# A fill of rounded products of ones, and a value tile ahead of the norm's product, in the head of a transformer-block kernel

## The reference

```python
def rmsnorm(x, g):
    xf = x.astype(jnp.float32)
    y = xf * lax.rsqrt(jnp.mean(xf * xf, axis=-1, keepdims=True) + EPS)
    return y * g.astype(jnp.float32)

h = rmsnorm(x, norm_attn[layer])
proj = h @ w_in[layer]
q_n, kv_n, g_n, qkv_s, g_m = jnp.split(proj, split_at, axis=-1)
...
# inside nsa_attention: keys and values of the compressed branch,
# an MLP over overlapping blocks of 32 tokens
kc = compress_blocks(k_c, *cmp_k)
vc = compress_blocks(v_c, *cmp_v)
...
bias_c = jnp.moveaxis(tbl[t5_bucket(dist_c)], (2, 3), (0, 1))
```

## Time and profile before

| | |
|---|---|
| time, median of 3 runs | 777.65 us (776.0 to 778.55) |
| the profiled execution's own time | 777.13 us |
| its span, first to last instruction | 775.3 us |
| TensorE busy | 764.9 us, 99% |
| VectorE, ScalarE, GpSimd busy | 498.7, 393.4, 279.6 us |
| share of the chain that ended last | TensorE 92%, VectorE 4%, ScalarE 2% |
| mean granted TensorE clock | 0.996 of 2.4 GHz |

### The profile page before, as it was taken

How to read it: one execution, slowest core, us unless ns; L and a number is a source line. 1 busy time by engine, 2 the same in 40 slices (tenths; PEclk the granted TensorE clock), 3 DMA queues, 4 the chain that set the end, 5 groups by cost and what they waited for, 6 DMA issues and landing times.

```text
span 775.3 us, 11284 instructions
## 1 busy us (share of the span) xinstructions
PE 764.9 (99%) x3956; PEld 632.2 (82%) x3956; DVE 498.7 (64%) x1025; ACT 393.4 (51%) x734; POOL 279.6 (36%) x366
## 2 busy tenths in 40 slices
PE   8999999999999999999999999999999999999996
PEld 6878888888877787778888888888888888888895
DVE  7546557787757676635444747787777777876334
ACT  6433324688966566565245654444444444443321
POOL 1255424511113332146556553333333322233630
PEclk9999999999999999999999999999999999999999
DMA  7963013210150111134332324322223333332213
GB/s 263 342 202 144 1 57 106 83 55 28 32 160 29 55 42 41 41 108 152 108 108 82 109 82 135 109 90 96 89 87 102 109 109 109 109 109 82 92 45 109
DMA packets 26003, 77.77 MB, mean 100 GB/s; under 512 B 3710, under 2 KB 6966, under 8 KB 25695
## 3 DMA queue, kind: packets, MB, share of 16 engines
q1 hardware_dynamic: 23868, 74.72, 29.4%
q10 hardware_dynamic: 2083, 2.37, 1.0%
HBM read 73.90 MB, written 2.13 MB: 98 GB/s over the span
## 4 chain that ended last, share of the span: by engine, by line
PE 92%; DVE 4%; ACT 2%; issue 1%; DMA 1%; POOL 0%; DVEq 0%; SPq 0%
PE bank L1568 31%; PE bank L1979 20%; PE bank L1951 10%; PE bank L1953 5%; PE bank L1885 2%; PE bank L1867 2%; PE bank L1799 2%; PE bank L1919 2%; PE bank L1923 2%; PE bank L1924 2%; PE bank L1844 1%; PE bank L1817 1%; PE bank L1580 1%; PE bank L1581 1%; PE bank L1582 1%; PE bank L1699 1%
## 5 line engine op out<-in xcount | busy, mean ns | idle before, releaser
L652 POOL TENSOR_TENSOR wlo<-wraw,whi 128x256 fp32r<-128x256 f32 x344 | 265.1, 803 | 455.4 <-ACT whi L693 372.7
L693 ACT ACTIVATE whi<-wraw 128x1024 fp32r<-128x1024 f32 x77 | 80.7, 1054 | 27.7 <-PE bank L1979 16.0
L1568 PE MATMUL bank<-hh,wlo 128*128 128x512 f32 x304 | 81.0, 396 | 0.7 <-DVE gm L1231 0.5
L1568 PE MATMUL bank<-hl,whi 128*128 128x512 f32 x304 | 80.6, 392 | 0.0
L1568 PE MATMUL bank<-hh,whi 128*128 128x512 f32 x304 | 79.6, 391 | 0.0
L1568 PEld LDWEIGHTS bank<-hh,whi 128*128 128x128 f32 x304 | 56.6, 188 | 11.7
L1568 PEld LDWEIGHTS bank<-hl,whi 128*128 128x128 f32 x304 | 56.4, 188 | 11.7 <-issue 0.2
L1568 PEld LDWEIGHTS bank<-hh,wlo 128*128 128x128 f32 x304 | 55.4, 188 | 12.8 <-DVE gm L1231 0.9
L1979 PE MATMUL bank<-r_l,whi 128*128 128x512 f32 x224 | 57.9, 390 | 0.0
L1979 PE MATMUL bank<-r_h,wlo 128*128 128x512 f32 x224 | 56.3, 392 | 0.0
L1979 PE MATMUL bank<-r_h,whi 128*128 128x512 f32 x224 | 55.7, 389 | 0.0
(11 more groups left out here) (316 smaller groups left out, 1611.6 us busy)
## 6 DMA issues: line engine op xcount, KB each, us to landing
wraw<-in_panels SPq DMA_DIRECT2D x101, 512.0 KB, 3.3
land<-in_panels SPq DMA_DIRECT2D x12, 512.0 KB, 4.5
w1k<-in_w SPq DMA_DIRECT2D x1, 2048.0 KB, 9.8
w1v<-in_w SPq DMA_DIRECT2D x1, 2048.0 KB, 15.0
svraw<-in_panels SPq DMA_DIRECT2D x4, 512.0 KB, 5.0
hank<-bias_by_distance SPq DMA_DIRECT2D x4, 512.0 KB, 6.4
x_res<-in_xT SPq DMA_DIRECT2D x4, 512.0 KB, 4.5
out_dram<-x_res SPq DMA_DIRECT2D x12, 128.0 KB, 1.8
```

The source lines that it names most:

```text
L652: ins = nc.gpsimd.tensor_tensor(wlo[:, s, k:k + 2], wraw[s][:, k:k + 2], whi[:, s, k:k + 2].bitcast(F32), ALU.subtract)
L693: A(whi[:, s], wraw[s][:], ACT.Copy).then_inc(w_hi, 1)
L1568: ins = M(b[:, cols], lhs, (xl if a == 1 else xh)[:, row + k, cols], start=(m == 0), stop=(m == 23))
```

## The change

The products of ones take the rounded tile `ones_r` instead of `ones`, wait for the fifth set-up signal (the cast that makes `ones_r`) and are 42 instead of 9. Three more stand between the first products of the first panel: one behind the first, two behind the second. On TensorE the third value tile comes ahead of `rms`; the order is now v0, v1, v2, rms, bias 0, bias 1, v3, rcol. On ScalarE the cast of panel 4 comes ahead of Ln and Exp; that of panel 5 stays behind them.

```diff
-WARM = 9
+WARM = 42
...
             A(oneh_r[:], oneh[:], ACT.Copy).then_inc(table_hi, 1)
+            split(4)
             ps = result(act, "rms")
             act.wait_ge(set_done, 4)
             emptied(A(rstd_b[:], ps[:], ACT.Ln, bias=epsc[:], scale=1.0 / D), "rms")
             stored(act, "rms")
             A(rstd_b[:], rstd_b[:], ACT.Exp, scale=-0.5).then_inc(rst, 1)
-            split(4)
             split(5)
             token_pairs(act, 0)
...
-            pe_.wait_ge(set_done, 1)
+            def product_of_ones():
+                M(bank[7][:, 0:P], ones_r[:], ones_r[:], start=True, stop=True)
+
+            pe_.wait_ge(set_done, 5)
             for i in range(WARM):
-                M(bank[7][:, 0:P], ones[:], ones[:], start=True, stop=True)
+                product_of_ones()
...
             for i in range(X_EARLY):
                 rounded(i)
+                for _ in range((1, 2, 0, 0, 0, 0)[i]):
+                    product_of_ones()
                 if i >= 1:
                     weight_low(i - 1)
...
             sparse_values(0)
             sparse_values(1)
+            sparse_values(2)
             b = claim(pe_, "rms")
...
             filled(ins, "rms")
             bias_rows(0)
-            sparse_values(2)
             bias_rows(1)
             sparse_values(3)
```

## The result

The changed kernel takes 780.91 us (median of 7 runs, 780.19 to 781.65) against 778.02 before (7 runs, 776.00 to 778.55): ratio 1.0044, 95% interval 1.0033 to 1.0054. By the ratio it is 3.4 us slower (the two medians are 2.9 apart), where 0.4 faster was foreseen; 780.91 lies beyond the range that was given, which ended at 779.6. The profiled execution takes 781.38 us, 4.25 above that of before, and its span 779.6 against 775.3.

The account below looks back on a forecast made before the run. TensorE, busy 99% of the span, was taken as the bound. Head gain, new order and later transfers summed to -0.94 + 0.10 + 0.4 = -0.44 us, from a median of 777.65 to 777.2; range 775.3 to 779.6.

Parts of the forecast that it names:

- Part 1: TensorE's fill at the head: 42 rounded products replace nine fp32 ones, running from about 1.5 to 7.4 us.
- If the clock rises at 5.01 again: Assumption for the fill: full clock from 5.01 us, as in the profile before, so the fill ends at 7.4 us.
- rival (c): Clock doesn't rise under the lighter fill: second panel 1.1 to 2.0 us later, 778.9 to 779.8 us; chance 0.12.
- I take 0.17: Spacing in us of the fill's rounded products at half clock, chosen between bounds of 0.17 and 0.21.
- The delay is absorbed: Fill overruns the first inputs by 1.2 to 1.6 us; products behind it still end before 12.50, costing nothing.
- the prize: Second panel's first product on TensorE starts at 12.50 instead of 13.44 if the clock stays full: 0.94 us gained.
- up to 781: Upper time in us if half clock at the head lasts beyond about 13 us.
- Rival (a), no gain: Timed runs may lack the clock's fall at 8.43, leaving nothing to win: 777.7 to 778.2 us; chance 0.22.
- Part 2: Three single products of ones between the first products: 0.33 us, absorbed, filling no gap if the fill ends at 7.4.
- Part 3: Third value tile ahead of the norm's product on TensorE: +0.10 us, including a new 0.38 wait for Ln.
- Part 4: Cast of panel 4 ahead of Ln on ScalarE, in its idle time: nothing gained, nothing lost.
- What is late next: Norm's delay through x2 transfers and block matrices to the compression's first layer: 0.4 us, between landings following issue or queue.

Follow-up runs that it names:

- fill_22: The changed kernel with 22 instead of 42 products of ones in the fill: 778.19 us, ratio 1.0015 to before.
- fill_only: The changed kernel with the old order on TensorE and ScalarE, keeping 42 rounded products and the three between: 781.19 us, ratio 1.0050 to before.
- narrow_22_old_order: The changed kernel with 22 fill products of 128 columns and the old order, the three between kept: 776.70 us, ratio 0.9989 to before.
- fill_22_wide: The changed kernel with 22 fill products, every product of ones streaming 256 columns instead of 128: 776.89 us, ratio 0.9995 to before.
- wide_42: The changed kernel with its products of ones widened from 128 to 256 columns, still 42 in the fill: 777.49 us, ratio 0.9998 to before.
- wide_22_no_between: The changed kernel with 22 fill products of 256 columns, the old order and no products between the first ones: 776.38 us, ratio 0.9988 to before.
- wide_22_old_order: The changed kernel with 22 fill products of 256 columns, the three between kept, and the old order: 776.61 us, ratio 0.9989 to before.
- fp32_12: The kernel before with 12 instead of 9 fp32 products of ones and nothing else: 776.45 us, ratio 0.9983 to before.
- cast_first: The kernel before with only ScalarE's cast of panel 4 moved ahead of Ln: 777.15 us, ratio 0.9999 to before.
- order_only: The kernel before with only the third value tile and the cast of panel 4 moved: 778.25 us, ratio 1.0012 to before.

## Why the prediction was wrong, point by point

**The step that failed** is in Part 1: "If the clock rises at 5.01 again". It didn't rise under the fill at all, so the fill ended at 10.50 and not at 7.4, and TensorE reached the second panel at 17.44 and not at 12.50. In the four traces with a fill of 128 columns (after, fill_22, fill_only, narrow_22_old_order) the first rise stands at 15.72, 10.85, 13.06 and 11.67, each behind 2.5 us or more of the first panel's products. In the four with 256 columns (fill_22_wide, wide_42, wide_22_no_between, wide_22_old_order) it stands at 5.10, 5.20, 4.78 and 4.89. wide_42 against the changed kernel makes this the cause and not a companion: one edit, 0.0044 of loss to 0.0002 of gain. What it is in the wider product that brings the rise, no run here separates. That was rival (c), with a chance of 0.12. I had the doubt in hand, that no row shows a rise under narrow rounded products, and gave the row of another kind of product, fp32, the weight of a precedent.

**A term mis-sized, in the same part.** "I take 0.17" for a rounded product at half clock: measured (10.50 - 1.48)/42 = 0.215, the other bound. The pair of loads 0.17 apart was the first of a burst, on an idle engine; back to back, the products stood as far apart as the fp32 records had. With a rise at 5.01 this would have been worth 0.4 us and hidden (the prediction gave 7.8 for it); without one it is 42 x 0.045 = 1.9 us of the fill's end. The 107 ns that the Trainium skill gives for such a load (TensorE: Matmul & The Clock Gate, section on LDWEIGHTS) no run here shows at half clock; the measured 0.215 us decides.

**Length and clock together.** "The delay is absorbed" was right for the case it was worked out for: wide_42's fill ended at 8.24, later than the 7.4 of the sum, and cost nothing against before that can be measured. It did cost the prize: the second panel started at 13.26. And the low clock alone cost little: narrow_22_old_order is not slower than before, whose own clock is half from 8.43 to 11.84. The loss needs both: a fill that runs 4.3 us past the first inputs, and half clock behind it. At full clock the 18 products take 4.1 us; from the fill's end to the second panel it took 6.9 in the changed kernel and 5.7 in fill_only. Rival (c) had this sum, but with the rise at 11.84 as in before, hence at most 2.0 us; the rise came at 15.72 and 13.06, so it was 4.0 and 2.8. The number said to bound it, "up to 781", held for the median.

**The prize** was right where the clock stayed up, the fill was short and the inputs came in time: 0.94 foreseen; 1.04, 1.20 and 0.90 in the second panel's start of fill_22_wide, wide_22_no_between and fp32_12. It was 0.62 in wide_22_old_order, where an input came late, and 0.18 in wide_42. In time, the ratios say 0.4, 0.9 and 1.3 us for the first three.

**Rival (a), no gain,** was partly right: executions differ. cast_first, whose head is that of before, had its rise at 13.51 instead of 5.01 and its second panel 0.8 us later. A before that is caught so has more to win.

**Part 2**: right that the three fill nothing by themselves; they also aren't needed.

**Part 3**: +0.10 foreseen, 0.20 measured in the changed kernel (4.20 - 4.00) and 0.18 in order_only (35.06 - 34.92 = 0.14, and its second panel had come 0.04 earlier). The new wait of 0.38 is there, as 0.32.

**Part 4**: nothing, as foreseen (cast_first).

**What is late next.** In the changed kernel itself there was no stall: TensorE was 4 us late. w1v was issued 4.0 us later than before, x2 7.1 us later (from 36.3), and x2 then landed faster (minimum, median, maximum us from issue) than in the earlier trace rows:

```profile
DMA to landing us min/median/max: 3.9/4.9/5.9
```

The block matrices began at 44.50, 3.3 us later than before. In order_only x2 was issued 3.0 us later (from 32.2) and the matrices began at 42.68, 1.5 later. So neither of the two rules in the prediction held, landings with the issue or with the queue alone: about half of the delay came through. With the head on time the 0.4 us was therefore low for the order alone: order_only shows 0.9 in its profile, and 0.9 in its ratio with the 0.2 of Part 3 in it. The wait ahead of the first layer comes and goes: 0.5 to 1.4 us in three of the five traces with the new order, 0.7 and 1.2 in two of the seven with the old, and none in the others.

## What to carry to other kernels

A fill is judged by when the clock rises in its own trace, not by the engine being busy: a stream of narrow products behind full weight loads kept TensorE occupied for 9 us and left it at half clock. Size a fill in products at half clock (0.21 us here for a rounded one of 128 or 256 columns, 0.43 for an fp32 one, which is two records) and let it end where the first inputs arrive; here such a fill that failed cost nothing against before in the old order (narrow_22_old_order). Where a trace lacks the very operation that a change adds, take both the nearest rows and the chance that the mechanism fails seriously: here both doubts were written down and both priced too low. And read the same head in more than one execution: the fp32 fill of before brought its early rise in two traces of three.

## What the runs showed of the hardware that I had not expected

- Rounded products of 128 and of 256 columns take the same time at half clock (0.215 and 0.21 us), and fp32 records of 128 columns too (0.21). Since 512 columns take 0.43, 256 of them account for 0.21 by themselves, but 128 for half of it: what holds the narrow product is something else, by the prediction its weight load, which no run separates. Under the 128-column one the clock rose in none of four traces; under the 256-column one in four of four, at 4.8 to 5.2 us; under nine fp32 products near 5 us in two (before, order_only at 4.64) and not in a third (cast_first); with twelve of them at 7.13 in one.
- A smaller gap ahead of the first product (0.99 us before and 1.41 in order_only, where the clock fell; none in wide_42 and fp32_12, 0.27 to 0.51 in the other three wide versions) goes with a clock that stays up. A gap alone doesn't bring it down: in fp32_12 it stayed up through 0.97 us idle before 8.32. What exactly keeps it up isn't separated: these fills also ended later.
- The time of the first rise differs between executions with the same work ahead of it by 2.7 us (13.06 and 15.72).
